# A trunk of two layers on one core: the feed-forward products are copied into an fp32r tile before TensorE transposes them

## The reference

```python
def swiglu_ffn(x, w_in, w_out):                 # w_in 1024 x 5632, w_out 2816 x 1024
    gate, up = jnp.split(x @ w_in, 2, axis=-1)
    return (jax.nn.silu(gate) * up) @ w_out

for i in range(2):
    x = x + 0.5 * swiglu_ffn(rms_norm(x, ffn1_norm[i]), ffn1_w_in[i], ffn1_w_out[i])
    x = x + mixer_i(rms_norm(x, mix_norm[i]))   # i = 0: pooling and convolution; i = 1: spatial gating
    x = x + 0.5 * swiglu_ffn(rms_norm(x, ffn2_norm[i]), ffn2_w_in[i], ffn2_w_out[i])
return rms_norm(x, final_norm)
```

## Time and profile before

| | |
|---|---|
| median of 3 runs | 928.09 us (928.08 to 928.15) |
| the profiled execution's own time | 928.09 us |
| its span, first to last instruction | 926.4 us |
| PE busy | 915.4 us (99%) |
| DVE busy | 524.5 us (57%) |
| ACT busy | 413.2 us (45%) |
| POOL busy | 23.9 us (3%) |
| mean granted TensorE clock | 0.999 |

### The profile page before, as it was taken

The page is one execution under the profiler, slowest core; times in us unless marked ns, Lnnn a source line. Parts: engine busy times, 40 slices in busy tenths (PEclk is TensorE's granted clock), DMA queues, the critical chain, the costliest instruction groups (busy, mean ns, idle before and its releaser), DMA issues.

```text
span 926.4 us, 11393 instructions
## 1 busy us (share of the span) xinstructions
PE 915.4 (99%) x4349; PEld 763.8 (82%) x4349; DVE 524.5 (57%) x511; ACT 413.2 (45%) x452; POOL 23.9 (3%) x44
## 2 busy tenths in 40 slices
PE   8999999999999999999999999999999999999997
PEld 7888888889878888888888888888899878888885
DVE  5645455458976554454565454545669464554543
ACT  5544244446844443443544434424564264434432
POOL 1400000000000000000000000000000000000000
PEclk9999999999999999999999999999999999999999
DMA  8955646725313856476527465566284276455531
GB/s 281 299 184 182 219 147 204 265 96 191 105 47 116 293 178 206 160 250 240 190 95 269 152 207 186 181 215 216 91 301 154 91 236 218 160 207 177 182 114 46
DMA packets 126668, 170.20 MB, mean 184 GB/s; under 512 B 5237, under 2 KB 111241, under 8 KB 126632
## 3 DMA queue, kind: packets, MB, share of 16 engines
q1 hardware_dynamic: 126632, 169.70, 54.3%
HBM read 168.63 MB, written 1.05 MB: 183 GB/s over the span
## 4 chain that ended last, share of the span: by engine, by line
PE 91%; DVE 6%; issue 1%; DMA 1%; ACT 1%; POOL 0%; SPq 0%; POOLq 0%; ACTq 0%; DVEq 0%
PE acc L964 10%; PE acc L962 10%; PE acc L963 10%; PE ga L962 10%; PE ga L964 10%; PE ga L963 10%; PE ub L964 9%; PE ub L962 9%; PE ub L963 9%; DVE xs L846 3%; PE tp L1066 2%; DVE w_lo L669 1%; PE tp L1023 1%; DMA raw<-in_ffn_w_in_dram 1%; ACT w_hi L454 0%
## 5 line engine op out<-in xcount | busy, mean ns | idle before, releaser
L669 DVE TENSOR_TENSOR w_lo<-raw,w_hi 128x2048 fp32r<-128x2048 f32 (+1 forms) x154 | 348.0, 2284 | 119.9 <-ACT w_hi L454 119.0
L454 ACT ACTIVATE w_hi<-raw 128x2048 fp32r<-128x2048 f32 (+1 forms) x154 | 289.1, 1904 | 33.6 <-DMA raw<-in_ffn_w_in_dram 21.0
L962 PE MATMUL acc<-w_hi,act_hi 128*128 128x512 f32 x416 | 163.4, 393 | 0.0
L964 PE MATMUL acc<-w_hi,act_lo 128*128 128x512 f32 x416 | 162.0, 389 | 0.0
L963 PE MATMUL acc<-w_lo,act_hi 128*128 128x512 f32 x416 | 161.9, 389 | 0.0
L962 PE MATMUL ga<-w_hi,xn_hi 128*128 128x512 f32 x384 | 155.0, 404 | 0.4 <-DVE w_lo L669 0.3
L964 PE MATMUL ga<-w_hi,xn_lo 128*128 128x512 f32 x384 | 150.1, 391 | 0.0
L963 PE MATMUL ga<-w_lo,xn_hi 128*128 128x512 f32 x384 | 149.8, 390 | 0.0
L964 PE MATMUL ub<-w_hi,xn_lo 128*128 128x512 f32 x384 | 149.6, 390 | 0.0
L962 PE MATMUL ub<-w_hi,xn_hi 128*128 128x512 f32 x384 | 149.5, 389 | 0.0
L963 PE MATMUL ub<-w_lo,xn_hi 128*128 128x512 f32 x384 | 149.5, 389 | 0.0
(11 more groups left out here) (133 smaller groups left out, 585.0 us busy)
## 6 DMA issues: line engine op xcount, KB each, us to landing
raw<-in_ffn_w_in_dram SPq DMA_DIRECT2D x176, 512.0 KB, 4.8
raw<-in_ffn_w_out_dram SPq DMA_DIRECT2D x88, 512.0 KB, 4.1
raw<-in_sgu_w_in_dram SPq DMA_DIRECT2D x16, 512.0 KB, 4.9
raw<-in_ab_w_in_dram SPq DMA_DIRECT2D x12, 512.0 KB, 4.6
raw<-in_ab_w_out_dram SPq DMA_DIRECT2D x8, 512.0 KB, 4.0
raw<-in_sgu_w_out_dram SPq DMA_DIRECT2D x8, 512.0 KB, 5.4
gain<-in_ffn_norm_dram SPq DMA_DIRECT2D x4, 512.0 KB, 5.8
xres<-in_x_dram SPq DMA_DIRECT2D x2, 512.0 KB, 5.8
```

The lines of the kernel that those rows point to most:

```text
L454: act.activation(w_hi[:, n % RING, o:], raw[:, n % RAW, o:], ACT.Copy).then_inc(hi_split, 1)
L669: dve.tensor_tensor(w_lo[:, n % RING, o:], raw[:, n % RAW, o:], w_hi[:, n % RING, o:].bitcast(F32), ALU.subtract).then_inc(lo_split, 1)
L962: pe.matmul(dst, s_hi, m_hi, start=start, stop=False)
L964: return pe.matmul(dst, s_lo, m_hi, start=False, stop=stop)
```

## The change

For the units 1 to 8 of each feed-forward stage the product is no longer transposed from `sgh`. ACT issues a transfer of 256 KB (`to_turn`) that copies `sgh[:, 1]` bit for bit into `turn[slot]`, two fp32r tiles laid over `act_lo[:, 6:8]` and `act_hi[:, 6:8]`. TensorE waits for `turn_landed` and transposes from there with an fp32r identity, `ident_r` (`turned_copy`). ACT makes `ident_r` from `ident` once, in stage 0, and TensorE waits for `ident_r_ready` after `first_unit`. The products of units 0, 9 and 10 are transposed as before. Which unit's product is transposed in which unit's place stays the same.

```diff
+        ident_r = sb("ident_r", [P, P], F32R)
...
+        turn = [act_lo[:, 6:8, :], act_hi[:, 6:8, :]]
+        TURNS = STEPS - 3
...
+            def to_turn(slot, f, i=None):
+
+                act.wait_ge(ga_free, at(f + 1, 2, i))
+                act.wait_ge(ub_free, at(f + 1, 2, i))
+                act.dma_start(turn[slot].bitcast(F32), sgh[:, 1, :, :]).then_inc(turn_landed, 16)
...
                     gate_rows(1, b, r, f, ACT.Silu)
                     split_to(b + 5)
+                    if k == 0:
+                        act.wait_ge(consts, CONSTS)
+                        act.activation(ident_r[:, :], ident[:, :], ACT.Copy).then_inc(ident_r_ready, 1)
                     with act.Fori(0, (STEPS - 3) // 2) as i:
                         for j in range(2):
...
                             gate_rows(1, n, r + s, f + s, ACT.Silu, i)
                             split(n + 5, i)
+                            to_turn(1 - j, f + s, i)
                             split(n + 6, i)
...
+            def turned_copy(bank, slot, c, i=None):
+
+                pe.wait_ge(turn_landed, at(16 * c, 32, i))
+                for j in range(2):
+                    for t in range(TT):
+                        o = j * T + t * P
+                        mm = pe.transpose(bank[:, o:o + P].bitcast(F32R), turn[slot][:, t, j * P:(j + 1) * P],
+                                          ident_r[:, :])
+                mm.then_inc(hidden_full, 1)
...
                 if kind == "ffn":
                     first_unit(k, f)
 
+                    c0 = e // STEPS * TURNS
+                    pe.wait_ge(ident_r_ready, 1)
+
...
                     def step(j, start, i=None):
                         n = b + 2 + 3 * j
-                        unit(n, f + 1 + j, i, lambda: turned(tp[j]))
+                        if j == 0 and i is None:
+                            unit(n, f + 1, None, lambda: turned(tp[0]))
+                        else:
+                            unit(n, f + 1 + j, i, lambda: turned_copy(tp[j], j, c0 + j, i))
                         step_out(n + 2, j, e + 1 + j, start, i)
...
-                        turned(tp[(s - 1) % 2])
+                        if s == STEPS - 2:
+                            turned_copy(tp[0], 0, c0 + TURNS)
+                        else:
+                            turned(tp[1])
```

More of the change, by code:

```diff
@@ L184, in hybrid_trunk @@
         gated = sem("gated")
+        ident_r_ready = sem("ident_r_ready")
+        turn_landed = sem("turn_landed")
         hidden_full = sem("hidden_full")
```

## The result

The changed kernel takes 933.09 us (median of 6 runs, 931.88 to 933.36), the kernel before 928.12 in the same comparison (927.9 to 928.76). The ratio is 1.005, interval 1.004 to 1.0061: 5.0 us slower, clear of the 0.2% that a measurement can tell. The profiled execution took 933.07 us.

A forecast was written before the change was run, and what follows sets the result against it. The prediction took TensorE's instruction stream to bound the kernel: 928.09 us, less 5.5 for cheaper transposes, plus 4.6 for the one-time identity wait, with transfer and clock at zero, gives 927.2 us; range 924.7 to 934.0.

The forecast's parts named there:

- the clock: TensorE's idle stretch after stage 0's first unit may drop its clock: nothing in the sum, 0 to 2.3 us in the range.
- the transposes: 128 feed-forward transposes in 32 groups step at 0.0667 us in fp32r instead of 0.110: 5.5 us saved.
- rival B: fp32r transposes step at 0.110 to 0.120 us because of their weight load, leaving the wait: 932.7 to 934.0 us; chance 0.24.
- What bounds the kernel: TensorE's instruction stream sets the time, PE busy 915.4 of 926.4 us; a microsecond there is one of the result.
- The wait for the identity: In stage 0 TensorE waits after unit 0 for ACT's identity copy, queued behind a gate and two slabs: 4.6 us lost once.
- The transfer: One copy per unit, 32 in all, issued by ACT behind a split, with 3 us of cover: cost zero.
- late copies: Rival: copies land late, or short fp32r operations cost four cycles a column (13 us more, 946 us); chance 0.04.
- C: Rival: an fp32r transpose step between, near 0.08 us up to 0.088, giving 928.9 to 929.9 us; chance 0.14.

The follow-up runs named there:

- the wait alone: Kernel before plus only the fp32r identity, made where the change makes it, and TensorE's wait for it; no transfer, transposes as before: 935.11 us.
- fp32-from-the-copy kernel: Early-identity kernel with the 128 changed transposes done in fp32 from the copied tile, same transfers and waits: 928.06 us.
- busy-in-the-wait kernel: Changed kernel with 18 fp32 matmuls of constants put between the first unit and the wait for the identity: 930.4 us.
- 64-column runs: Early-identity kernel with three extra 64-column transposes behind the first of each group: 940.98 us with fp32r extras, 940.55 us with fp32 extras.
- doubled groups: Early-identity kernel with every changed transpose issued twice into the same place, eight per group instead of four: 936.9 us.
- copy behind both splits: Early-identity kernel with each unit's transfer issued after the second of ACT's two splits instead of between them: 928.34 us.
- early-identity kernel: Changed kernel with ACT making the fp32r identity before the first gate of stage 0, TensorE's wait left in place: 925.78 us.

## Why the prediction was wrong

The forecast was 927.2 and no measurable change; the kernel takes 933.1 and is 5 us slower. Of the 5.9 us between the two, the clock is 2.7, which stood in the sum as nothing, and the transposes are 3.2, priced at 5.5 saved where they save 2.3. That the time still lies inside the range of 924.7 to 934.0 is luck: the upper end came from rival B, in which the transposes gain nothing and the clock stays up, and neither happened. Point by point:

**What bounds the kernel:** right. A microsecond put into TensorE's stream, or taken from it, is one of the result: the wait alone costs the kernel before 7.0 us, the type of the transposes is worth 2.3 by the fp32-from-the-copy kernel, and 928.1 + 7.0 - 2.3 = 932.8 us, measured 933.1. None of the runs behind these two figures is one of the changed kernel.

**The wait for the identity:** right in mechanism and size. Predicted 4.6 us, with ACT's copy ending near 30.21 and unit 1 starting at 30.37; the copy ended at 30.37 and the unit started at 30.42, 4.43 us late, and the busy-in-the-wait kernel prices it at 4.6. ACT's activation into `ident_r` took 0.30, not 0.39.

**The clock:** the first step that failed. I named the fall, bounded it by 0 to 2.3 us and took nothing in the sum, without a reason for nothing, though the idle stretch was longer than the 4.1 us at the end of the trace after which the clock had fallen. One row is one case: at the ends of the ten profiled executions the clock fell between 2.3 and 5.3 us after PE's last matmul, and in the two idle stretches of 4.3 us it fell after 3.1 and 3.9. It cost 2.7 us by the experiment, above my upper bound. That bound came from a warm-up that had not run at the low clock throughout: twice the 3.29 us of the fast one would be 6.6, and it took 5.56.

**The transposes:** the second step that failed, a term mis-sized more than twofold: 5.5 us predicted, 2.3 measured. Two things were wrong in it. The step of an fp32r transpose is 0.085 us, not the 0.0667 of the line through the matmuls of 256 and 512 columns; the 64-column runs show that it does not shrink with the columns, so a line in columns was the wrong model. What sets it stays open. The reason that I had given for the upper end, a load of 188 ns, did not come about: the loads of the fp32r transposes are recorded at 139 ns, as those in fp32 are the earlier trace rows. And only three of a group's four steps get shorter: from the last transpose to the next matmul it is 0.11 us in either kernel. 32 x 3 x 0.025 = 2.4 us. I had multiplied by four.

The figure of the Trainium skill (TensorE: Matmul & The Clock Gate, section Back-to-back issue gap), about 81 ns a matmul of 128 columns in a stream of loads and matmuls, agrees with the 0.085 us of the doubled groups. By it alone the saving, as an estimate, was 3.7 us, still with four steps instead of three.

**The transfer:** right at zero, and the fp32-from-the-copy kernel shows it (928.06 against 928.08). Two details were wrong. I let the copy go out when the first split ends and delay the second by the issue; it goes out 0.09 us after the product is finished, while that split still runs, and delays nothing, so a steady unit has 4.8 us of cover and not 3. And the first unit of a stage's loop can have less, as the copy behind both splits shows. I had late copies as a rival for all units alike; ACT's waits for slabs are the places to look at.

**The rivals:** the outcome is none of them alone. Nearest is C, the step in between (0.080 to 0.088, 928.9 to 929.9 us), with the clock's fall on top, which makes 931.6 to 932.6; what is still missing is the fourth step, which saves nothing. The rival with no gain from the transposes gives nearly the same time, 932.7 to 934.0, and the total alone could not have told the two apart; the early-identity kernel does.

## What to carry to other kernels

On a saturated engine, price a one-time wait like a change to the inner loop: here one 0.3 us instruction, placed behind two that nobody waited for, outweighed 128 cheaper ones, and moving it turned +0.5% into -0.25%. When TensorE will stand for about as long as a trace shows it standing before a lower clock, put the low clock into the sum, not only into the range. Count a saving by the steps that can shorten: here the step from the last short operation of a group to the long one behind it stayed at 0.11 us.

## What the runs showed of the hardware

- An fp32r transpose of 128 x 128 follows another by 0.085 us, an fp32 one by 0.11; with 64 moving columns 0.082 and 0.06. The recorded weight load is 0.14 us in both types, so its duration does not tell them apart.
- From the last of these transposes to the 512-column fp32r matmul behind it the step is 0.11 us in both types, and after four or eight transposes alike.
- Where operands went from 128 to 64 rows, the next weight load came some 0.15 us later than otherwise, and on the way back some 0.1; a group with three small transposes cost 0.2 us more than their steps.
- An idle stretch of about 4.3 us brought TensorE's clock to 1.2 GHz in both profiled executions that had it, after 3.1 and 3.9 us of it, and the low clock then lasted 13 matmul steps in one and 7 in the other: beyond the standing, the same wait cost 2.7 us and 1.45 us.
- 32 transfers of 256 KB within SBUF, 8.4 MB beside 170 MB of loads, changed no time of a steady unit (16.80 us with fp32 transposes, with and without them). They landed 4.6 us after the issue by the median and 5.9 at the longest in the changed kernel, 6.6 at the longest in the one with the copy behind both splits; such an issue goes out of ACT's queue while an activation issued before it is still running.
